# Square output products of a two-block transformer: 512 moving columns from two weight slots in place of 256 from one

## What is computed

```python
mix_out = jnp.einsum('bsd,de->bse', merged, w_out[l])       # out1
h = h + rms_norm(mix_out, norm_mix_post[l])
...
return o.reshape(b, s, MLA_HEADS * MLA_V) @ w_o             # out2, x = x + y
...
return out.astype(h.dtype) @ w_o                            # out3, x = x + y
```

## Time and profile before

| | us |
|---|---|
| device time, median of 2 runs | 2282.18 (2280.25 to 2284.1) |
| span of the profiled execution | 2278.1 |
| PE busy in it | 2131.4 (94%) |
| PEld busy | 1818.3 (80%) |
| DVE busy | 963.5 (42%) |
| ACT busy | 830.5 (36%) |

### The profile page before, as it was taken

One profiled execution on the slowest core, in us unless ns is written; L12 is line 12 of the kernel. 1 busy time (PEld: TensorE's weight loads), 2 busy tenths in 40 slices (PEclk: granted clock), 3 DMA queues, 4 the chain that ended last, 5 costly groups with the idle time before them and its releaser, 6 DMA issues. The chain is left out here.

```text
span 2278.1 us, 27535 instructions
## 1 busy us (share of the span) xinstructions
PE 2131.4 (94%) x11313; PEld 1818.3 (80%) x11313; DVE 963.5 (42%) x1315; ACT 830.5 (36%) x1132; POOL 0.2 (0%) x4
## 2 busy tenths in 40 slices
PE   6899999999799999878888899999999978999999
PEld 5688888788788888777677888888779878888887
DVE  3544543233544434445653434434433334344343
ACT  4222332322432333336564343333344443423332
POOL 0000000000000000000000000000000000000000
PEclk9999999999899999988898999999999989999999
DMA  5222212123133222211011222332222212223222
GB/s 183 66 78 63 65 49 72 56 93 102 57 100 105 97 92 92 67 39 42 20 38 38 74 93 93 106 96 92 78 71 75 75 38 75 92 93 109 92 92 76
DMA packets 168319, 178.51 MB, mean 78 GB/s; under 512 B 5921, under 2 KB 138606, under 8 KB 168114
## 3 DMA queue, kind: packets, MB, share of 16 engines
q1 hardware_dynamic: 168088, 177.36, 24.6%
q10 hardware_dynamic: 154, 0.04, 0.0%
HBM read 175.29 MB, written 2.10 MB: 78 GB/s over the span
## 5 line engine op out<-in xcount | busy, mean ns | idle before, releaser
L83 PE MATMUL psum<-norm_T_hi,weights_hi 128*128 128x512 f32 x1184 | 469.1, 396 | 13.9 <-PEq L435 6.4
L85 PE MATMUL psum<-norm_T_hi,weights_lo 128*128 128x512 f32 x1184 | 462.0, 390 | 0.0
L84 PE MATMUL psum<-norm_T_lo,weights_hi 128*128 128x512 f32 x1184 | 461.8, 390 | 0.0
L83 PE MATMUL psum<-weights_hi,act_T_hi 128*128 128x512 f32 (+2 forms) x976 | 369.1, 378 | 8.4 <-DVE weights_lo L286 4.1
L84 PE MATMUL psum<-weights_lo,act_T_hi 128*128 128x512 f32 (+2 forms) x976 | 367.4, 376 | 0.0
L85 PE MATMUL psum<-weights_hi,act_T_lo 128*128 128x512 f32 (+2 forms) x976 | 367.2, 376 | 0.0
L1014 ACT ACTIVATE weights_hi<-raw_weights 128x2048 fp32r<-128x2048 f32 x96 | 183.5, 1911 | 359.7 <-PE psum L85 359.7
L83 PE MATMUL psum<-weights_hi,norm_T_hi 128*128 128x256 f32 (+2 forms) x928 | 267.9, 289 | 9.1 <-PEq L784 4.1
L83 PEld LDWEIGHTS psum<-norm_T_hi,weights_hi 128*128 128x128 f32 x1184 | 223.0, 188 | 64.8 <-issue 14.5
L1035 DVE TENSOR_TENSOR weights_lo<-raw_weights,weights_hi 128x2048 fp32r<-128x2048 f32 x96 | 220.1, 2293 | 111.3 <-ACT weights_hi L1014 111.1
L84 PE MATMUL psum<-weights_lo,norm_T_hi 128*128 128x256 f32 (+2 forms) x928 | 262.8, 283 | 0.0
(11 more groups left out here) (229 smaller groups left out, 1990.3 us busy)
## 6 DMA issues: line engine op xcount, KB each, us to landing
raw_weights<-in_ffn_w_dram SPq DMA_DIRECT2D x64, 1024.0 KB, 5.2
raw_weights<-in_w_in_dram SPq DMA_DIRECT2D x36, 512.0 KB, 4.5
raw_weights<-in_w_up_dram SPq DMA_DIRECT2D x16, 1024.0 KB, 5.4
raw_weights<-in_w_down_dram SPq DMA_DIRECT2D x16, 1024.0 KB, 5.1
raw_weights<-in_w_in_dram SPq DMA_DIRECT2D x12, 1024.0 KB, 5.1
raw_weights<-in_mlstm_w_in_dram SPq DMA_DIRECT2D x8, 1024.0 KB, 5.2
raw_weights<-in_w_out_dram SPq DMA_DIRECT2D x4, 1024.0 KB, 5.8
raw_weights<-in_mla_w_o_dram SPq DMA_DIRECT2D x4, 1024.0 KB, 5.3
```

The lines of the kernel that those rows point to most:

```text
L83: pe.matmul(out, ah, bh, start=start, stop=False)
L84: pe.matmul(out, ah, bl, start=False, stop=False)
L85: return pe.matmul(out, al, bh, start=False, stop=stop)
```

## The change

Two consecutive units of a square weight now serve one pass. TensorE waits until both are split (`w_lo` at u0 + 2 * hh + 2), and each matmul streams 256 columns from slot 0 and 256 from slot 1, as one moving operand `WH[:, :, w]` or `WL[:, :, w]` of 2 x 256, into a whole bank of 512. So that slot 0 always holds the left 256 columns of a half, `square` exchanges the two units of a pair where the first unit number is odd. There are 192 matmuls of 512 columns in a product in place of 384 of 256. A pair of units has 4 groups, all on its first unit, and the consumers count accordingly. The order of ScalarE's and VectorE's instructions is unchanged.

```diff
@@ -130,8 +130,10 @@
 
     def square(name, w):
         at[name] = len(units)
+        first = at[name] % 2
         for j in range(4):
-            add(4, kpn(w)[:, :, 256 * j:256 * j + 256])
+            c = j ^ first
+            add(4 if j % 2 == 0 else 0, kpn(w)[:, :, 256 * c:256 * c + 256])
 
     def ffn(name, up, down):
         at[name] = len(units)
@@ -890,11 +892,15 @@
 
                 @block.tensor
                 def _(pe):
-                    for j in range(4):
-                        pe.wait_ge(w_lo, u0 + j + 1)
+                    for hh in range(2):
+                        pe.wait_ge(w_lo, u0 + 2 * hh + 2)
                         for t in range(NT):
-                            group_N(pe, u0 + j, 0, 256, 256, KD,
-                                    PS[:, 4 * (j // 2) + t, 256 * (j % 2):256 * (j % 2) + 256], t, srch, srcl)
+                            for k in range(KD):
+                                w = slice(k * 256, k * 256 + 256)
+                                tt = slice(t * P, t * P + P)
+                                mm = mm3(pe, PS[:, 4 * hh + t, :], srch[:, k, tt], srcl[:, k, tt],
+                                         WH[:, :, w], WL[:, :, w], k == 0, k == KD - 1)
+                            mm.then_inc(gemm, 1)
 
                 @block.scalar
                 def _(act):
@@ -903,7 +909,7 @@
                     if gain is not None:
                         for hh in range(2):
                             for t in range(NT):
-                                act.wait_ge(gemm, gb + 8 * hh + 4 + t + 1)
+                                act.wait_ge(gemm, gb + 4 * hh + t + 1)
                                 if hh or t:
                                     act.wait_ge(sq.sem, sq.at(4 * hh + t))
                                 act.activation(JUNK, PS[:, 4 * hh + t, :], ACT.Square,
@@ -933,7 +939,7 @@
                         if gain is not None:
                             dve.scalar_tensor_tensor(x, TMP[:, n, :], rstd[:, t:t + 1], x, MUL, ADD).then_inc(resid.sem, 1)
                         else:
-                            dve.wait_ge(gemm, gb + 8 * hh + 4 + t + 1)
+                            dve.wait_ge(gemm, gb + 4 * hh + t + 1)
                             dve.tensor_tensor(x, PS[:, n, :], x, ADD).then_inc(resid.sem, 1)
             resid.passed(8)
             if gain is not None:
```

## The result

The changed kernel takes 2339.54 us (median of 2 runs, 2338.79 to 2340.29) against 2282.18 us for the kernel before. The ratio is 1.0246 with a 95% interval of 1.0227 to 1.0265 (the two medians alone divide to 1.0251), so it is 2.5% slower. The forecast was 2340 us. A later measurement of the same kernel gave 2341.95 us and 1.0262 (1.0241 to 1.0283). Ratios leave out three slow runs of the kernel before, of 2475 us and more. The profiled execution has 2338.5 us against 2278.1 us, 60.4 us more.

The account below looks back on a forecast made before the run. TensorE's own work and its waits were taken to make the time. Terms 12.8 + 0.7 + 20.0 + 6.8 + 24.0 - 6.8 = 57.5 us gave 2335.6 us profiled, about 2340 us timed, range 2328 to 2350.

Parts of the forecast that it names:

- Spacings and the saving: Output products: at full clock one wide matmul (0.2267 us) replaces two narrow (0.240), saving 6.8 us over 510.
- Two-slot read: Wide matmuls' operand from both slots: between 0.2267 and 0.240 us each; the lower end was taken.
- the rival with 0.240: Output products: reading two slots costs extra, 0.240 us per wide matmul, nothing saved, 2346 us; chance 0.10.
- the one with 0.120: Output products: a wide matmul costs hardly more than a narrow one, 0.120 us, giving 2279 us; chance 0.02.
- the rival of covered stalls: Output products: part of the stalls is covered, 12 us less than the sum, time within 2%; chance 0.05.
- the one of a held clock: Middle of each product: the clock holds or is back almost at once, 49.6 us added, 2332 us; chance 0.08.
- Opening: Start of each product: TensorE waits for u0+1 too, 4.27 us each, 12.8 us; 0.7 more in the first product.
- Middle: Between each product's halves: refills wait for both slots, 20.0 us of stall, plus 6.8 us of low clock behind.
- Tail: End of each product: u0+4's split waits for the last matmul, the evacuation queued behind it; 24.0 us, largest term.
- From profile to time: Whole kernel: 2335.6 us in a profile, timed runs 4.1 above it, so 2339.7, say 2340 us.
- the two-slot rival with long slow stretches: Two-slot reads cost extra and slow stretches are the long ones too: up to 2352 us; within the rival's chance 0.10.
- the rival of a cheap wide matmul: Output products: weight loads set the pace, so wide matmuls at 0.120 us save 61 us more, 2279 us; chance 0.02.

Follow-up runs that it names:

- the second profile: The changed kernel, unedited, profiled and timed once more: 2341.95 us, ratio 1.0262 to the kernel before.
- narrow ones on the same waits: Changed kernel with all its waits, each wide matmul made as two of 256 columns, one from each slot: 2348.54 us, ratio 1.0288.
- measured alone the stages grow by 12.4: Kernel before, narrow matmuls kept, TensorE waiting for both units u0 and u0+1 at each output product's opening: 2299.66 us, ratio 1.0071.
- the filled stalls: Changed kernel with 28 unneeded matmuls of 512 columns run on TensorE in each middle stall: 2334.22 us, ratio 1.0228.
- Together measured alone: Kernel before; split of u0+2 waits for both first quarters, TensorE for u0+3 before the third: 2310.32 us, ratio 1.0121.
- alone 24.6 in the stages: Kernel before, split of u0+4 waiting until the last quarter is multiplied, evacuation behind it in both queues: 2311.72 us, ratio 1.0123.

## Why the prediction was right

- *What bounds it*: right. The work of VectorE and ScalarE stayed the same to 1 us (963.5 and 962.6, 830.5 and 830.1); what changed is what it waits for.
- *Spacings and the saving*: 0.0133 us for each of 510 wide matmuls, 6.8 us; measured 6.4 (7.4 by the second profile) against narrow ones on the same waits. The low-clock spacing of 0.427 was an estimate and was measured as 0.427.
- *Two-slot read*: the lower end was right, 0.2267 us. By this the rival with 0.240 falls, and so does the one with 0.120. With every stall at its forecast length, the rival of covered stalls falls too, and with the clock at 0.50 behind the middle stall the one of a held clock. The Trainium skill's 131 ns for 512 columns ("TensorE: Matmul & The Clock Gate", "Back-to-back issue gap") isn't met by the changed kernel either.
- *Opening*: 12.8 for the stalls; the three gaps are 13.0 us longer, and measured alone the stages grow by 12.4. The 0.7 for the first product was wrong. I had taken a slow stretch of 4.8 us behind the stall in place of 3.4. But the clock fell already in the idling, at about 545.2 us, and was back at 552.0, so of the matmuls, which begin at 548.85, only 3.15 us were slow. Alone this opening cost 4.24 us.
- *Middle*: 20.0 for the stall and 6.8 for the clock. The stall is 6.59 us of idling plus 0.39 less 0.23, hence 6.75, three times 20.3, and the filled stalls give 6.1 for the clock. Together measured alone 26.1 against 26.3. The Trainium skill's rule ("TensorE: Matmul & The Clock Gate", section "Why this matters for your kernels"), that such a gap loses the clock, agrees with the clock of 0.50 in the first microseconds behind the gap shown above.
- *Tail*: 24.0; alone 24.6 in the stages and 24.0 in the transposes' three waits behind them; 24.2 in these waits of the changed kernel. Naming what was queued behind the fourth split was the step that carried most.
- *Sum*: 57.5 against 56.6 in the stages of the first pair of profiles, 55.6 if the changed kernel's second profile is taken. The terms as measured one by one give 13.0 + 20.3 + 6.1 + 24.2 - 6.4 = 57.2.
- *From profile to time*: here an error was hidden, and luck covered it. The timed runs' excess over the profile was taken as 4.1 us, from before's own profile and median. It was 1.0 in the first profile of the change, and 4.1 because that profile of before was a low one. In the other direction the rest, taken as unchanged, came out 3.8 us longer than in that profile. The two cancel. In a profile the forecast was 2335.6, 2.9 short of 2338.5. That 2339.7 met 2339.54 to 0.2 us is chance, with two runs on each side and a later measurement of 2341.95; that it was within some 3 us is not.
- *Two slips in the rivals*, neither of them in the sum or the range: the price of the two-slot rival with long slow stretches is not 2352, since 64.3 + 0.7 us give 2347. And the rival of a cheap wide matmul gets even with the kernel before at 0.127 us (57 us saved, not 55), but the time would have been within 2% already at 0.206 us (12 us saved). The measured 0.2267 is above both.

## What to carry to other kernels

An instruction that reads both halves of a double buffer at once takes the double buffering away: each refill then waits until both are free. What must be priced is not the instruction but the refill's chain (here 6.7 us in each product), the clock behind the gap (2.0 us), and everything queued behind the refill on the other engines (8 us). Saving 0.0133 us on a matmul is worth having only if another buffer takes over; look for one that the stage leaves idle, and start with what is ready. And when a change should be worth a few us, compare the stages in the traces and take more than one profile of before.

## What the runs showed that I had not expected

Two executions of the same program have spans of 2278.1 and 2283.7 us, and 5.5 us of difference lie in the attention stretch, by how long the clock stands at half in it: 0.83 to 0.86 against 0.90 to 0.93 over 100 us with the same matmuls. Where matmuls are dense the executions agree: in the feed-forward behind out2, SyncE's loads at 1315.54 and at 1596.46 us of the first profile are 280.92 us apart in all three profiles of before. And the three costs are additive within the noise of about 1 us (63.1 against 63.0), although each moves the point at which the next begins.
